# Expert gate and up weights laid line d to partition d / 8 instead of line d to partition d mod 128

## What is computed

```
logits = h @ router_w + router_b
top_v, top_i = top_k(logits, 2); gates = softmax(top_v) spread over the 8 experts
for e in range(8):
    y += gates[:, e:e+1] * ((silu(h @ w_gate[e]) * (h @ w_up[e])) @ w_down[e])
```

## Time and profile before

| | |
|---|---|
| median of 3 runs | 1684.69 us (1680.78 to 1685.04) |
| the profiled execution | 1678.34 us |
| its span, first to last instruction | 1676.6 us |
| mean granted TensorE clock in it | 0.992 of full speed |
| moved by DMA | 462.53 MB in 102849 packets |

### The profile page before, as it was taken

How to read it: one execution, slowest core, us unless ns; L and a number is a source line. 1 busy time by engine, 2 the same in 40 slices (tenths; PEclk the granted TensorE clock), 3 DMA queues, 4 the chain that set the end, 5 groups by cost and what they waited for, 6 DMA issues and landing times.

```text
span 1676.6 us, 40077 instructions
## 1 busy us (share of the span) xinstructions
PE 1610.4 (96%) x18395; PEld 1069.6 (64%) x18395; DVE 506.2 (30%) x960; ACT 221.2 (13%) x463; POOL 52.0 (3%) x126
## 2 busy tenths in 40 slices
PE   8999999999999999999999999999889998899987
PEld 6888878999999888788834444354333543335433
DVE  1456233776633347424221110202002020020201
ACT  2324111100001415211110000000000000000001
POOL 4000200000000000200000000000000000000000
PEclk9999999999999999999989999999999999999999
DMA  9342225444542531223799999999999999999995
GB/s 263 126 151 101 78 78 181 171 163 141 202 143 76 176 137 65 102 89 115 297 402 362 389 409 425 428 425 425 427 427 426 425 426 426 427 428 416 425 426 237
DMA packets 102849, 462.53 MB, mean 276 GB/s; under 512 B 9932, under 2 KB 20862, under 8 KB 78110
## 3 DMA queue, kind: packets, MB, share of 16 engines
q1 hardware_dynamic: 102686, 459.99, 69.3%
HBM read 458.92 MB, written 1.05 MB: 274 GB/s over the span
## 4 chain that ended last, share of the span: by engine, by line
PE 87%; DMA 12%; issue 1%; ACT 0%; DVE 0%; SPq 0%; DVEq 0%
PE bank L1273 24%; PE bank L489 20%; PE bank L1290 12%; DMA slot<-in_moe_w_down 11%; PE bank L1062 8%; PE bank L1147 4%; PE bank L1014 3%; PE bank L850 2%; PE bank L970 2%; PE bank L1207 1%; PE bank L803 1%; PE bank L1217 1%; PE bank L531 1%; DMA slot<-in_w_in 1%; PE bank L483 1%
## 5 line engine op out<-in xcount | busy, mean ns | idle before, releaser
L1273 PE MATMUL bank<-slot,xg 128*32 128x512 f32 (+1 forms) x4976 | 477.9, 541 | 14.2 <-DMA slot<-in_moe_w_up 8.2
L1273 PEld LDWEIGHTS bank<-slot,xg 128*32 128x32 f32 x4976 | 159.4, 110 | 322.9 <-issue 291.6
L489 PE MATMUL bank<-h,slot 128*128 128x256 f32 x1440 | 324.4, 383 | 3.3 <-issue 3.3
L489 PEld LDWEIGHTS bank<-h,slot 128*128 128x128 f32 x1440 | 271.0, 191 | 46.4 <-issue 10.4
L1290 PE MATMUL bank<-slot,aT 128*32 128x256 f32 x4408 | 248.3, 383 | 24.7 <-DMA slot<-in_moe_w_down 24.3
L1290 PEld LDWEIGHTS bank<-slot,aT 128*32 128x32 f32 x4408 | 142.5, 111 | 130.1 <-DMA slot<-in_moe_w_down 30.6
L2703 DVE TENSOR_TENSOR av<-gs,bank 128x512 f32<-128x512 f32 (+1 forms) x40 | 38.2, 954 | 517.9 <-PE bank L1273 517.9
L1979 ACT ACTIVATE gs<-bank 128x512 f32<-128x512 f32 (+1 forms) x40 | 21.8, 544 | 399.1 <-PE bank L1273 399.1
L1014 PE MATMUL bank<-sq,slot 128*128 128x256 f32 x256 | 55.9, 379 | 0.0
L1984 ACT ACTIVATE SpT<-bank 128x512 f32<-128x512 f32 x8 | 4.8, 598 | 382.7 <-PE bank L1303 382.7
L1014 PEld LDWEIGHTS bank<-sq,slot 128*128 128x128 f32 x256 | 48.5, 190 | 6.5
(11 more groups left out here) (502 smaller groups left out, 1468.5 us busy)
## 6 DMA issues: line engine op xcount, KB each, us to landing
slot<-in_moe_w_gate SPq DMA_DIRECT2D x32, 2048.0 KB, 23.0
slot<-in_moe_w_up SPq DMA_DIRECT2D x32, 2048.0 KB, 27.5
slot<-in_moe_w_down SPq DMA_DIRECT2D x32, 2048.0 KB, 25.7
slot<-in_moe_w_up SPq DMA_DIRECT2D x31, 1536.0 KB, 25.6
slot<-in_moe_w_down SPq DMA_DIRECT2D x31, 1536.0 KB, 22.4
slot<-in_moe_w_gate SPq DMA_DIRECT2D x30, 1536.0 KB, 25.5
slot<-in_w_in SPq DMA_DIRECT2D x18, 2048.0 KB, 7.9
slot<-in_ffn_w_up SPq DMA_DIRECT2D x5, 2048.0 KB, 7.6
```

The costliest lines, as they stand in the source:

```text
L489: ins = mm(o, w[:, k, c:c + n], rhs[:, k, :], start=k == 0, stop=k == nk - 1)
L1273: ins = mm(o.rearrange("s (q x) -> s q x", q=4), xg[:, g, k, :], rows_of(w[:, kk, :], p), start=k == 0, stop=k == KD - 1)
```

## The change

Matrix line d of an expert's gate and up matrices now goes to partition d / 8 and block d mod 8. The two blocks of one load are then two neighbouring lines of the matrix for each partition. The pieces stay as long as they were (8 KB and 6 KB, since a load takes 2048 or 1536 of 3584 columns), and there are as many. The distance in HBM between the lines of neighbouring partitions goes from one line (14,336 bytes) to eight (114,688 bytes), and between a partition's two pieces from 128 lines to one.

The gather follows: quarter q, c and block b of column d = 256q + 8c + b. The matmul still sends b outside and c inside, and so it now reads 32 elements that are 8 elements (32 bytes) apart, goes one element on, and reads 32 more, eight times over. Its output in PSUM, `xg` and all else keep their places. The down matrices, the router and the dense layer are as they were.

```diff
@@ gather's columns
             def strip(t, p):
 
-                return t.rearrange("r (b q c) -> r q b c", q=4, c=32)[:, p]
+                return t.rearrange("r (q c b) -> r q b c", q=4, c=32)[:, p]
@@ loads
-            mg = a["moe_w_gate"][0].rearrange("e (k p) n -> e p k n", p=P)
-            mu = a["moe_w_up"][0].rearrange("e (k p) n -> e p k n", p=P)
+            mg = a["moe_w_gate"][0].rearrange("e (p k) n -> e p k n", p=P)
+            mu = a["moe_w_up"][0].rearrange("e (p k) n -> e p k n", p=P)
             md = a["moe_w_down"][0]
```

## The result

The changed kernel takes 1683.73 us (median of 18 runs) against 1681.13 us for the kernel before (median of 18 runs). One run of the changed kernel took 5904.85 us in a slow state and is left out of the ratio, which is 1.0017, 95% interval 1.0010 to 1.0024. So the change costs 2.9 us, between 1.7 and 4.0 us (the two medians lie 2.6 us apart). The forecast was +2.6 us. That is under the 0.3% that was taken for the limit of such a measurement; with 18 runs of each it can be told from nothing.

A forecast was written before the change was run, and what follows sets the result against it. TensorE was taken to bound 847 to 1000 us, DMA loads the stretch after. Loads 0, first gather 1.5, second 1.1 and later gathers 0 gave +2.6 us on the 1684.69 median, 1687.3 us; range 1679 to 1700.

The forecast's parts named there:

- Two stretches with two bounds: 847 to 1000 us: slower TensorE moves the end equally; 1000 to 1655: hidden by 39 us idle and 12 us queue.
- The loads, 0: Gate and up loads at the new HBM pitch cost 0; bounds 11 us less to 16 us more.
- The gather's factor, 1.57 from VectorE's row: Gather matmuls reading 32-byte steps slow by 1.57, from VectorE's strided write of 1074 ns against 682 straight.
- First gather, +1.5 as the middle of 0 and 3.0: Gather at 841.8 to 847.1 us, mostly 1.2 GHz: 3.0 us more by clock cycles, 0 by memory's own time.
- the prediction's second case: First gather: price in memory's own time, 2.73 x 1.57 = 4.3 us, under 5.28, so nothing is added.
- Second gather, +1.1: Gather at 956.27 us, where TensorE never idles: 1.86 x 0.57 = 1.1 us more.
- The sum, +2.6: Whole kernel: loads 0, first gather 1.5, second 1.1, later gathers 0, together +2.6 us.
- The later gathers, 0: Third to eighth gather, after 1000 us: 7.9 us more work, hidden under 39 us of idle time, cost 0.
- Rival A: Costly stride in the gathers, factor near 4: +11 to +21 us, 1696 to 1706; chance 0.25.
- its point of decision: Rival A decides from about factor 2.2 on, where the two early gathers cost over 5 us.

The follow-up runs named there:

- the early stride: Kernel before with only the first two gathers reading elements 32 bytes apart, loads as before: ratio 1.0025 (1.0012 to 1.0038), +4.2 us.

## Why the prediction came out, step by step

- **Two stretches with two bounds.** Right. Added work before 1000 us counted 8.1 us for 8.3. Added work after it was hidden to some nine tenths, so "costs nothing" was a little too strong. The idle time of TensorE after 1000 us was forecast to fall to 31 us and fell to 29, but that agreement is luck: the later gathers added 14.7 us and not 7.9, and the idle time fell by 10 of them.
- **The loads, 0.** Right, shown by the loads alone (1.0001) and by unchanged GB/s after 1000 us. The argument, that two placings so different gave one rate already in before, held.
- **The gather's factor, 1.57 from VectorE's row.** Too low: 2.04 to 2.08 in the gathers. The ratio of a VectorE write was no measure for a TensorE read. The row and the Trainium skill's rule ("Advanced Engine Details and Errata", section "SBUF Cachelines") pointed the same way, and the rule was right about where the price starts (632 ns a record at 16 bytes against 388 at 8).
- **First gather, +1.5 as the middle of 0 and 3.0.** The measured +0.47 lies near the lower end. A record took 5.75 us / 48 = 120 ns mostly at 1.2 GHz and 3.80 us / 32 = 119 ns at 2.4 GHz, so the strided read has a pace of its own, and the slow clock had already paid for most of it. Within the first gather of the changed kernel, four records (one for each quarter) start every 0.47 us, before the clock rose at 846.5 us as after it; with neighbours it is every 0.43 us at 1.2 GHz and 0.22 at 2.4 (before). So the prediction's second case, the memory's own time, was the nearer one. In the executions with neighbours the first gather took from 4.27 us (loads alone) to 5.28 (before), by when within it the clock rose; with the stride it took 5.75 or 5.76 in the changed kernel, the gather alone and the early stride. So the price is 0.5 to 1.5 us by execution.
- **Second gather, +1.1.** Measured +1.94, the size of the factor.
- **The sum, +2.6.** The trace gives 2.4, and with the cheaper first gathers up to 3.4; the runs gave 2.9. It came out so near because the factor was too low and the share of the first gather too high. One error covered the other.
- **The later gathers, 0.** Mostly right. The six later ones alone measured +1.9 us, interval 0 to 3.9, and three times the later gathers cost 3.2 us for 25.9. Whether 1 or 2 us of the change are theirs stays open.
- **Rival A**, a factor near 4, did not come, but its point of decision, put at a factor of about 2.2, was not far from the measured 2.05. What kept the price small was the pace of the strided read at the first gather. Had the price gone by clock cycles there, the factor of 2.05 would have cost 5.28 x 1.05 = 5.5 us in the first gather and 7.5 us with the second, over the 5 us. With the pace that was measured, the two pass 5 us only from a factor of about 2.65 (2.73 x 2.65 - 5.28 + 1.86 x 1.65).

## What to carry to other kernels

When a layout is changed for the sake of a load, look first at what the reader of the other operand must now do: here a TensorE moving operand with one float32 element in each 16 bytes streamed at half speed at 2.4 GHz (a gather took 5.60 us instead of 2.73), while 8-byte steps were nearly free (2.85 us). Place each touched instruction in time before pricing it; here two of eight gathers carried the loss that could be shown. And a load in pieces of 6 KB and more, already at 425 GB/s, did not care which line went where.

## What the runs showed of the hardware that was not expected

- The price of a strided float32 read by TensorE is a step between 8 and 16 bytes: a gather of three groups took 2.73 us with neighbours and 2.85, 5.60 and 5.67 us with steps of 8, 16 and 32 bytes. The factor was 2.1 in one stream (216 to 453 ns from record to record) as in four (57 to 119 ns), at 2.4 GHz. The strided gather took the same 120 ns a record mostly at 1.2 GHz as at 2.4 GHz (119), so at the slower clock it cost little.
- Matmuls written in a row for one quarter of the array ran at 58 ns a record when two in a row were for one quarter and others for other quarters followed, and at 216 ns when sixteen in a row were for one quarter. There the records stand out of program order in the trace.
- In two kernels with more matmuls in some gathers TensorE paused at the start of the last item (2.39 and 2.80 us) and waited for nothing visible; the cause is open. With 20.9 us of loads queued the rate stayed at 400 GB/s or more, with 13.8 us it fell to 324.
